# Sixteen-token projections: from one product of 256 columns to four of 64 in separate column groups of the array

## Chip, cores and metric

One NeuronCore of one Trainium2 chip runs the whole program. The metric is device time in microseconds (us), the median of several executions; one execution was also profiled. The work is done by TensorE (the 128x128 matrix array), VectorE, ScalarE and GpSimd; SyncE issues the transfers. In the profile these are PE, DVE, ACT, POOL and SP.

## What is computed

A batch of one with 256 tokens of width 1024 in float32 runs through two transformer blocks. The first block puts 16 learned "meta" tokens ahead of the 256, so that it works on 272 tokens, and has two layers. Each layer normalises the tokens, multiplies them by one wide input matrix, runs three kinds of attention (latent attention with 8 heads, stick-breaking attention with 8 heads, differential attention with 4 heads), merges them through gates, and ends with a feed-forward part. The second block has an attention mixer, a delta-rule mixer and two mixtures of 64 experts. The change touches only some projections of the first block:

```python
proj = h @ w_in[layer]
(c_q, c_kv, k_rope, sb_q, sb_k, sb_v,
 df_q, df_k, df_v, gate_logits) = _split_cols(proj, IN_SIZES)
```

The parts `sb_v` (the values of the stick-breaking attention) and `df_q`, `df_k`, `df_v` (queries, keys and values of the differential attention) are 512 columns wide each, and are the ones computed with tokens on the partitions.

## The kernel before

**Layout.** Activations lie as H[128 features, 8 blocks of features, 272 tokens]. The tokens are cut into three tiles, `TILES = [(0, 16), (16, 128), (144, 128)]`: the first tile is the 16 meta tokens (`META = 16`). Weights are streamed from memory in slots of 1 MB, each 256 output columns wide for all 1024 features, through a ring of four slots (`wdense`), which SyncE fills in a fixed order as TensorE is done with them.

**Two kinds of projection.** `feature_steps` (line 511) makes weights stationary and streams the tokens, and gives features on the partitions; the gates use it. `token_steps` (line 527) makes the tokens stationary and streams the weights, and gives tokens on the partitions. For each slot it goes through the three tiles of tokens. For each tile it takes a PSUM bank and runs 8 products (one for each block of 128 features), which accumulate into `o[0:n, 0:256]` (line 533, through `sum_k`, line 502). For the tile of 16 tokens the stationary operand is 128x16 and the moving one 128x256. In the trace each product in float32 is a pair of MATMULs with a LDWEIGHTS each, so this tile is 16 MATMULs "128*16 128x256". (A row of the timeline that shows x32 of them merges a 16-token tile and the tile of 128 tokens behind it, under the shape of the first.) Below, one such tile of one slot is called a *16-token step*.

**How many.** `sb_v`, `dq`, `dk` and `dv` take two slots each, so a layer has 8 such steps and the program has 16. The later mixers call `token_steps` with tiles of 128 tokens only.

**Who takes the results out.** The two tiles with an even number (the 16 tokens among them) are copied out of PSUM by VectorE in `even_tokens` (line 1327), the odd one by ScalarE in `odd_tokens`. `bank` (line 479) makes TensorE wait until the bank's last reader is through; eight banks rotate.

**The order of the work.** It is written out by hand, as generators that each engine advances alike. These projections are laid beside the attention heads, to fill TensorE while VectorE and ScalarE work on the probabilities. For head h of the latent attention, TensorE computes the scores of head h, advances the list `beside` by `BESIDE_MLA[h]` steps, and then transposes and applies the probabilities of head h-1. The two 16-token steps of `sb_v` come with heads 0 and 3. The stick-breaking heads do the same with `BESIDE_SB = (4, 4, 4, 4, 4, 5, 5, 6, 6)` over this list (`beside_sb`, line 347):

```python
yield from in_turn((dq, 6), (dk, 6), (rope_dq, 1), (gate, 1), (dv, 1), (gate, 1), (rope_dq, 1), (dv, 1), (gate, 1),
                   (dv, 1), (rope_dq, 1), (gate, 1), (dv, 1), (rope_dk, 1), (gate, 1), ...
```

So the 16-token steps of `dq` both come with head 0, the two of `dk` with heads 1 and 2, the first of `dv` with head 3, the second of `dv` with head 5. `rope_dq` and `rope_dk` are work of VectorE and ScalarE (the normalisation and rotation of DQ and DK, `norm_rope`, lines 1335 to 1362); TensorE does nothing in them.

**Applying probabilities.** `apply_v` (line 554) transposes the probabilities of a head (line 477), waits for VectorE to copy the 16-token part out of PSUM (`turned`, line 1378) and for ScalarE to copy the rest (line 2215), and then multiplies by the values.

Of the kernel before, what the change touches and what calls it, by code (L numbers as in the profile page):

```python
# [17 lines left out]
META = 16  # L18
# [5 lines left out]
TILES = [(0, META), (META, P), (META + P, P)]  # L24
# [212 lines left out]
def build(nc, io, out_ap, known):  # L237
    te, ve, ac, po, sp = nc.tensor, nc.vector, nc.scalar, nc.gpsimd, nc.sync
# [36 lines left out]
    def flat(a, n, *dims):  # L275
        ap = a[:, 0:n]
        if len(dims) == 1:
            return ap.rearrange("p (a b) -> p a b", a=dims[0])
        if len(dims) == 2:
            return ap.rearrange("p (a b c) -> p a b c", a=dims[0], b=dims[1])  # L280
        return ap
# [23 lines left out]
    def ps(*what):  # L305
        return PS[:, bank_of.get(what, 0), :]
# [18 lines left out]
    SVT = flat(wm_flat[:, 8 * T:], 1536, 3, 8)  # L325
# [15 lines left out]
    def in_turn(*order):  # L341

        for steps, n in order:
            for _ in range(n):
                yield next(steps, None)
# [117 lines left out]
    def tensor_program():  # L463
        PE, VE, AC = PES[0], VES[0], ACS[0]
# [6 lines left out]
        def mm(out, lhsT, rhs, start=True, stop=True):  # L471
            return te.matmul(out, lhsT, rhs, start=start, stop=stop, skip_group_check=True)  # L472
# [6 lines left out]
        def bank(what, *readers):  # L479

            while turn[0] % 8 in held:
                turn[0] += 1
            b = turn[0] % 8
            turn[0] += 1
            for done, label in owed[b]:
                te.wait_ge(done.sem, done.of(*label))
            owed[b] = [(done, what) for done in readers]
            assert what not in bank_of, what
            bank_of[what] = b
            return PS[:, b, :]  # L490

        def take(k, w):
            n = uses[0]
            uses[0] += 1
            te.wait_ge(*dense.landed(n))
            return dense.slot(n, k, w)

        def used(n=None):

            dense_at[uses[0] - 1 if n is None else n] = (PES.index(PE), PE.n)  # L500

        def sum_k(out, lhs, rhs, more=True):
            for j, (a, b) in enumerate(zip(lhs, rhs)):
                m = mm(out, a, b, start=j == 0, stop=j == len(lhs) - 1)
            return m
# [21 lines left out]
        def token_steps(what, src, kc, tiles, n_slots, readers, step=256):  # L527
            for s in range(n_slots):
                use, slot = uses[0], take(kc, step)
                for t, (t0, n) in enumerate(tiles):  # L530
                    label = what + (s, t)
                    o = bank(label, readers(t))
                    PE.up(sum_k(o[0:n, 0:step], [src[:, k, t0:t0 + n] for k in range(kc)],
                                [slot[:, k, :] for k in range(kc)]), *label)
                    if t == len(tiles) - 1:
                        used(use)
                    yield
# [36 lines left out]
        def first_layer(L):  # L574
# [27 lines left out]
            used()  # L602
            sb_qk = feature_steps(("sb qk", L), H, DC, T, 4, lambda j: AC)
            sb_v = token_steps(("sb v", L), H, DC, TILES, 2, lambda t: reader(t))
            gate = feature_steps(("gate", L), H[:, :, lo:T], DC, T - lo, 12, lambda j: AC if j < 2 else reader(j))
            advance(sb_qk, 1)
# [53 lines left out]
            def turned_to_feature(what, TMt, roped):  # L660
                te.wait_ge(VE.sem, VE.of("roped", roped, L))
                yield from to_feature((what, L), TMt.rearrange("p t h d -> p t (h d)"), 4, 128, lambda g: reader(g))

            tokens = lambda what: token_steps((what, L), H, DC, TILES, 2, lambda t: reader(t))
            beside = beside_sb(tokens("dq"), tokens("dk"), tokens("dv"), no_products(), no_products(), gate,
                               turned_to_feature("dqt", DQ, "dq"), turned_to_feature("dkt", DK, "dk"))
# [143 lines left out]
        def even_mixer():  # L810
# [70 lines left out]
            def moba():  # L881
# [31 lines left out]
                for h in range(4):  # L913
# [8 lines left out]
            run(even_order(gla(), moba(), norm_heads(("gla",), 1, [E_MIX[:, 4:8, :]]),  # L922
                           feature_steps(("mq",), H, DC, S, 2, both), feature_steps(("mk",), H, DC, S, 2, both),
                           token_steps(("mv",), H, DC, T2, 2, both), token_steps(("gv",), H, DC, T2, 2, both),
                           feature_steps(("gg",), H, DC, S, 2, both)))

# [368 lines left out]
        PE, VE, AC = PES[1], VES[1], ACS[1]  # L1295
# [3 lines left out]
        PE, VE, AC = PES[2], VES[2], ACS[2]  # L1299
# [4 lines left out]
    def vector_program():  # L1304
        PE, VE, AC = PES[0], VES[0], ACS[0]
# [5 lines left out]
        def copy(what, dst, src):  # L1311
            ve.wait_ge(PE.sem, PE.of(*what))
            VE.up(ve.tensor_copy(dst, src), *what)  # L1313
# [10 lines left out]
                    copy(what + (c,), *dst(c, ps(*what, c)))  # L1324
                yield

        def even_tokens(what, n_slots, tiles, dst):
            for s in range(n_slots):
                for t, (t0, n) in enumerate(tiles):
                    if t % 2 == 0:  # L1330
                        copy(what + (s, t), *dst(s, t, ps(*what, s, t)[0:n, 0:256]))
                    yield

# [63 lines left out]
        def first_layer(L):  # L1397
# [54 lines left out]
            for g in range(0, 8, 2):  # L1452
                copy(("kt", L, g), KT[0:96, g, :], ps("kt", L, g)[0:96, 0:T])

            sb_v = even_tokens(("sb v", L), 2, TILES, lambda s, t, o: (
                SVT[0:TILES[t][1], t, 4 * s:4 * s + 4, :], o.rearrange("p (h d) -> p h d", h=4)))
            beside = in_turn((sb_v, 3), (gate, 1), (sb_v, 3), (gate, 5))
            for h in range(MLA_H + 1):
                if h < MLA_H:
                    p, s = WA[h % 2], 10 * (h % 2)  # L1460
# [11 lines left out]

            def put(what, dst):
                fl = dst.rearrange("p t h d -> p t (h d)")
                return even_tokens((what, L), 2, TILES, lambda s, t, o: (fl[0:TILES[t][1], t, 256 * s:256 * s + 256], o))

            beside = beside_sb(
                put("dq", DQ), put("dk", DK), put("dv", DV),
                norm_rope("dq", DQ, row("diff_q_norm_g", 64 * L, 64 * L + 64), 64, 0, cst("df_cos"), cst("df_sin"), ROPE_D, L),
                norm_rope("dk", DK, row("diff_k_norm_g", 64 * L, 64 * L + 64), 64, 0, cst("df_cos"), cst("df_sin"), ROPE_D, L),  # L1480
# [5 lines left out]
            for h in range(SB_H + 1):  # L1486
                if h < SB_H:
                    z, e, lk, a = [WA[4 * (h % 2) + j] for j in range(4)]
                    what = ("sb", L, h)
# [46 lines left out]
            for br in range(3):  # L1536
                ve.wait_ge(AC.sem, AC.of("gates", L, br))
                for c in range(8):
                    what = ("branch", L, br, c)
                    o = ps(*what)[:, lo:T]  # L1540
# [9 lines left out]
            for c in range(8):  # L1550
                what = ("attended", L, c)
# [103 lines left out]
        def even_mixer():  # L1655
# [114 lines left out]
            def heads():  # L1770
# [9 lines left out]

            run(even_order(gla(), moba(), heads(), even_steps(("mq",), 4, fm(E_MQ)), even_steps(("mk",), 4, fm(E_MK)),
                           even_tokens(("mv",), 2, T2, tm(E_MV)), even_tokens(("gv",), 2, T2, tm(E_GV)), even_steps(("gg",), 4, fm(E_GG))))
            mix_out(0, "even out")
            layer_norm("even ln", modulated(0, "moe h", 0))
# [399 lines left out]
        for L in range(DEPTH):  # L2184
            first_layer(L)
# [10 lines left out]
        PE, VE, AC = PES[1], VES[1], ACS[1]  # L2196
# [3 lines left out]
        PE, VE, AC = PES[2], VES[2], ACS[2]  # L2200
# [738 lines left out]
```

## Time and profile before

| | |
|---|---|
| three timed runs | 3070.38, 3071.52 and 3080.09 us, median 3071.52 us |
| the profiled execution | 3072.53 us |
| its span, first to last instruction | 3071.2 us |
| mean granted TensorE clock | 0.968 of 2.4 GHz |
| TensorE matmul busy | 94% of the span, 16294 MATMULs |
| VectorE, ScalarE busy | 36%, 16% |

The profile is one execution. Times in it count from the first instruction. A row of the timeline gives the start, the length, the engine, the line, the operands and the number of instructions merged in it; in brackets stands how long the engine was idle before it, and what it waited for. "128*16 128x256" is a stationary operand of 128 rows and 16 columns against 256 moving columns.

### The profile page before, as it was taken

What the parts mean: (1) busy time and instruction counts of PE and PEld (TensorE: products, weight loads), DVE (VectorE), ACT (ScalarE), POOL (GpSimd) and SP (SyncE); (2) the same over time, 40 slices, a digit from 0 to 9 for tenths busy, and PEclk for the clock granted to TensorE, in tenths of its full rate; (3) what the DMA queues carried; (4) which work ended last, traced back from release to release, by engine and by line L of the source; (5) the groups of instructions that cost most, each with busy time, mean ns of one, the idle gap of its engine ahead of it and who ended that gap; (6) DMA issues with size and microseconds to landing.
All of it is one profiled execution on the core that took longest, in us unless ns stands there. A gap on an engine that the chain in (4) does not pass through costs nothing.

```text
span 3071.2 us, 41806 instructions
## 1 busy us (share of the span) xinstructions
PE 2883.4 (94%) x16294; PEld 2040.4 (66%) x16294; DVE 1115.9 (36%) x2516; ACT 487.2 (16%) x1066; POOL 102.7 (3%) x98
## 2 busy tenths in 40 slices
PE   7998899999999889999999999999899999999998
PEld 5666678787666678887875555555788765555554
DVE  2425424442534433543335222222564244222223
ACT  2212221000212221000211111111232111111111
POOL 0000000000000000000001000000000010000000
PEclk9998899999999899999999999999999889999999
DMA  5221135654221135664518999999231349999995
GB/s 187 82 82 69 55 123 208 248 214 149 96 83 69 69 110 213 233 240 178 214 70 334 394 399 382 400 402 390 101 124 57 123 185 403 402 405 399 400 403 218
DMA packets 104983, 684.45 MB, mean 223 GB/s; under 512 B 17760, under 2 KB 19312, under 8 KB 24496
## 3 DMA queue, kind: packets, MB, share of 16 engines
q1 hardware_dynamic: 93040, 665.02, 55.4%
q0 software_dynamic: 11264, 16.54, 1.5%
q8 instruction: 75, 1.23, 0.2%
q10 hardware_dynamic: 576, 1.43, 0.1%
q14 instruction: 28, 0.23, 0.0%
HBM read 703.37 MB, written 4.19 MB: 230 GB/s over the span
## 4 chain that ended last, share of the span: by engine, by line
PE 81%; DMA 11%; DVE 4%; ACT 2%; issue 1%; SPq 0%; DVEq 0%; ACTq 0%; POOLq 0%
PE PS L472 77%; DMA wmoe<-in_experts 10%; PE PS L477 4%; ACT AR L2215 1%; ACT AR L2265 1%; DMA COLS<-in_cols 0%; SPq L2823 0%; DVE ST L1371 0%; ACT ST L2215 0%; DVE X L1628 0%; DMA AR<-tokens,IX 0%; DVE AR L1521 0%; DVE AR L1368 0%; DVE wmoe L1391 0%; DVE AR L1519 0%
## 5 line engine op out<-in xcount | busy, mean ns | idle before, releaser
L472 PE MATMUL PS<-wmoe,AR 128*64 128x256 f32 (+2 forms) x5488 | 723.0, 420 | 35.7 <-DMA wmoe<-in_experts 22.5
L472 PE MATMUL PS<-H,wdense 128*128 128x256 f32 (+1 forms) x3056 | 719.6, 396 | 6.8 <-DVE H L1401 3.5
L472 PEld LDWEIGHTS PS<-H,wdense 128*128 128x128 f32 x3056 | 589.4, 195 | 116.2 <-issue 13.1
L472 PEld LDWEIGHTS PS<-wmoe,AR 128*64 128x64 f32 (+1 forms) x5488 | 388.9, 137 | 322.7 <-issue 148.3
L2215 ACT ACTIVATE AR<-PS 128x512 f32<-128x512 f32 (+7 forms) x497 | 227.1, 462 | 1624.5 <-PE PS L472 1023.8
L472 PE MATMUL PS<-AR,wdense 128*128 128x256 f32 (+1 forms) x1920 | 440.7, 389 | 21.3 <-DVE X L1591 6.4
L472 PE MATMUL PS<-AR 128*128 128x512 f32 (+16 forms) x1636 | 402.3, 395 | 40.3 <-DVE AR L1378 16.1
L472 PEld LDWEIGHTS PS<-AR,wdense 128*128 128x128 f32 x1920 | 367.4, 192 | 87.6 <-issue 20.4
L472 PEld LDWEIGHTS PS<-AR 128*128 128x128 f32 (+5 forms) x1636 | 214.0, 186 | 140.9 <-issue 92.6
L477 PEld LDWEIGHTS PS<-CST,AR 128*128 128x128 f32 (+3 forms) x1150 | 129.5, 134 | 159.5 <-issue 137.8
L472 PE MATMUL PS<-wdense,H 128*128 128x256 f32 (+4 forms) x1024 | 225.2, 376 | 2.5 <-DVE H L1635 2.2
L472 PEld LDWEIGHTS PS<-wdense,H 128*128 128x128 f32 (+1 forms) x1024 | 162.1, 171 | 56.7 <-issue 11.6
L477 PE MATMUL PS<-CST,AR 128*128 128x128 f32 (+3 forms) x1150 | 188.2, 275 | 6.0 <-DVE AR L2166 3.2
L1391 DVE SCALAR_TENSOR_TENSOR wmoe<-wmoe,CA 128x256 f32<-128x256 f32 x336 | 162.9, 485 | 12.0
L2129 DVE TENSOR_TENSOR AR<-AR,PS 128x256 f32<-128x256 f32 x67 | 28.2, 422 | 376.4 <-ACT AR L2215 376.4
L2135 DVE COPY AR<-PS 128x512 f32<-128x512 f32 x130 | 89.9, 692 | 135.1 <-PE PS L472 135.1
L2733 POOL DMA_INDIRECT AR<-tokens,IX x71 | 79.9, 1126 | 1056.0 <-DVE IX L2055 1005.5
L2215 ACT ACTIVATE AR<-AR 128x432 f32<-128x432 f32 (+8 forms) x111 | 76.7, 706 | 172.2 <-DVE AR L1491 83.9
L2119 DVE TENSOR_SCALAR AR<-AR 64x256 f32<-64x256 f32 x134 | 55.1, 411 | 104.3 <-PE PS L477 95.3
L1313 DVE COPY AR<-PS 128x256 f32<-128x256 f32 (+8 forms) x79 | 35.3, 448 | 152.6 <-PE PS L472 121.8
L472 PE MATMUL PS<-AR,CST 128*128 128x256 f32 (+4 forms) x212 | 62.3, 429 | 27.7 <-DMA COLS<-in_cols 15.9
L2215 ACT ACTIVATE AR<-X 128x256 f32<-128x256 f32 (+3 forms) x54 | 22.6, 462 | 346.5 <-DVE X L1591 132.9
(271 smaller groups left out, 1399.7 us busy)
## 6 DMA issues: line engine op xcount, KB each, us to landing
wmoe<-in_experts SPq DMA_DIRECT2D x402, 1024.0 KB, 9.0
wdense<-in_dense SPq DMA_DIRECT2D x176, 1024.0 KB, 4.8
wmoe<-in_ada SPq DMA_DIRECT2D x48, 1024.0 KB, 6.9
tokens<-AR POOLq DMA_DIRECT2D x4, 512.0 KB, 2.9
wdense<-in_dense SPq DMA_DIRECT2D x2, 768.0 KB, 10.5
wdense<-in_dense SPq DMA_DIRECT2D x2, 640.0 KB, 6.3
CST<-in_const SPq DMA_DIRECT2D x1, 1197.0 KB, 19.2
AR<-tokens,IX POOLq DMA_INDIRECT x71, 7.8
```

The source lines that it names most:

```text
L472: return te.matmul(out, lhsT, rhs, start=start, stop=stop, skip_group_check=True)
L477: return te.matmul(out, src, ident[0:n, 0:n], start=True, stop=True, is_transpose=True, skip_group_check=True)
L1313: VE.up(ve.tensor_copy(dst, src), *what)
L1391: VE.up(ve.scalar_tensor_tensor(ACC[:, s], WM[:, s, 256 * k:256 * k + 256], CA[:, k:k + 1], ACC[:, s], ALU.mult, ALU.add))
L2119: VE.up(ve.tensor_scalar(M_PWT[half].rearrange("p t s -> p (t s)"), M_NUM[half], M_IW[half, bass.ds(p, 1), 0], M_IW[half, bass.ds(p, 1), 1 ...
L2129: VE.up(ve.tensor_tensor(M_HM, M_HM, PS[:, B_GU, 0:256], ALU.mult))
L2135: VE.up(ve.tensor_copy(M_YE[:, q, :], PS[:, B_D[q], :]), *what, "ye", q)
L2215: return ac.activation(dst, src, f, bias=bias, scale=scale)
L2265: AC.up(ac.activation(p[:, o:o + w], p[:, o:o + w], Exp, bias=ST[:, s + j:s + j + 1], scale=1.0, accum_out=ST[:, s + 3 + j:s + 4 + j]))
L2733: po.indirect_dma_start(M_XT, None, tokens[L], bass.IndirectOffsetOnAxis(M_IX[:, column:column + 1], 0), bounds_check=SEQ - 1, oob_is_err= ...
```

## The change

For a tile of 16 tokens, the product with 256 weight columns becomes four products with 64 columns each. Product a writes its 16 rows at PSUM partitions 32a to 32a+15, that is from the a-th group of 32 columns of the array, and at columns 0 to 63 of the bank. The stationary operand (the 16 tokens) is loaded for each of them. Within each block of features the four follow one another. VectorE then takes the result out with four copies of 16x64, one from each range of partitions, where it had one of 16x256; they land in the same places as before. The tiles of 128 tokens and all else stay as they were.

```diff
@@ token_steps
-                    PE.up(sum_k(o[0:n, 0:step], [src[:, k, t0:t0 + n] for k in range(kc)],
-                                [slot[:, k, :] for k in range(kc)]), *label)
+                    if n == META:
+                        for k in range(kc):
+                            for a in range(4):
+                                m = mm(o[32 * a:32 * a + n, 0:step // 4], src[:, k, t0:t0 + n], slot[:, k, step // 4 * a:step // 4 * (a + 1)],
+                                       start=k == 0, stop=k == kc - 1)
+                        PE.up(m, *label)
+                    else:
+                        PE.up(sum_k(o[0:n, 0:step], [src[:, k, t0:t0 + n] for k in range(kc)],
+                                    [slot[:, k, :] for k in range(kc)]), *label)
@@ even_tokens, in the vector program
-        def even_tokens(what, n_slots, tiles, dst):
+        def even_tokens(what, n_slots, tiles, dst, quarter=None):
...
-                    if t % 2 == 0:
+                    if n == META:
+                        ve.wait_ge(PE.sem, PE.of(*what, s, t))
+                        for a in range(4):
+                            VE.up(ve.tensor_copy(quarter(s, a), ps(*what, s, t)[32 * a:32 * a + n, 0:64]))
+                        VE.mark(*what, s, t)
+                    elif t % 2 == 0:
                         copy(what + (s, t), *dst(s, t, ps(*what, s, t)[0:n, 0:256]))
@@ its callers
-                SVT[0:TILES[t][1], t, 4 * s:4 * s + 4, :], o.rearrange("p (h d) -> p h d", h=4)))
+                SVT[0:TILES[t][1], t, 4 * s:4 * s + 4, :], o.rearrange("p (h d) -> p h d", h=4)), lambda s, a: SVT[0:META, 0, 4 * s + a, :])
...
-                return even_tokens((what, L), 2, TILES, lambda s, t, o: (fl[0:TILES[t][1], t, 256 * s:256 * s + 256], o))
+                return even_tokens((what, L), 2, TILES, lambda s, t, o: (fl[0:TILES[t][1], t, 256 * s:256 * s + 256], o),
+                                   lambda s, a: fl[0:META, 0, 256 * s + 64 * a:256 * s + 64 * (a + 1)])
```

## Rows read from the trace of the kernel before

**Rows 1.** The page's chain that ended last, share of the span by engine.

```profile
PE 81%; DMA 11%; DVE 4%; ACT 2%; issue 1%; SPq 0%; DVEq 0%; ACTq 0%; POOLq 0%
```

**Rows 2.** Groups of matmuls by shape, whole span: count | busy us, mean ns | idle before.

```profile
L472 PE MATMUL PS<-wmoe,AR 128*64 128x256 f32 x4288 | 477.7, 381 | 1.5 <-ACT AR L2215 1.4
L472 PE MATMUL PS<-H,wdense 128*128 128x256 f32 x1792 | 411.0, 389 | 1.6 <-DVE H L1562 1.6
L472 PE MATMUL PS<-wdense,H 128*16 128x256 f32 x256 | 59.7, 388 | 0.0
```

**Rows 3.** TensorE's timeline beside latent head 3 and stick-breaking heads 0 and 1, layer 0.

```profile
123.13 7.28 PE L472 MATMUL PS<-wdense,H 128*16 128x256 f32 x32
130.25 0.97 PE L477 MATMUL PS<-CST,AR 128*16 128x128 f32 x6
...
175.93 15.97 PE L472 MATMUL PS<-wdense,H 128*16 128x256 f32 x64
191.83 1.10 PE L472 MATMUL PS<-wmoe 64*128 64x272 f32 x6
...
207.07 0.97 PE L477 MATMUL PS<-CST,AR 128*16 128x128 f32 x6
```

**Rows 4.** TensorE's timeline of both later mixers: 64-column products in several parts of the array.

```profile
1469.37 0.47 PE L472 MATMUL PS<-AR 64*64 64x64 f32 x16
1469.77 3.72 PE L472 MATMUL PS<-wdense,H 128*128 128x256 f32 x16
...
2282.38 3.95 PE L472 MATMUL PS<-AR 128*64 128x64 f32 x128
```

**Rows 5.** VectorE's copies out of PSUM by shape, whole span.

```profile
L2056 DVE COPY AR<-PS 128x3 f32 x55 | 8.9, 161 | 0.0
L1313 DVE COPY AR<-PS 16x256 f32<-16x256 f32 x13 | 5.3, 408 | 15.5 <-PE PS L472 15.5
```

**Rows 6.** Timeline beside stick-breaking head 3: VectorE, ScalarE in layer 0; VectorE, ScalarE in layer 1.

```profile
239.89 0.40 DVE L1313 COPY AR<-PS 16x256 f32<-16x256 f32 x1
241.55 0.43 DVE L1378 COPY AR<-PS 16x272 f32<-16x272 f32 x1 [1.26 <-PE PS L477]
...
240.74 0.49 ACT L2215 ACTIVATE wmoe<-PS,COLS 128x272 f32<-128x272 f32 x1 [0.57 <-PE PS L472]
241.55 0.49 ACT L2215 ACTIVATE AR<-PS 128x384 f32<-128x384 f32 x1 [0.32 <-PE PS L477]
...
957.37 0.43 DVE L1378 COPY AR<-PS 16x272 f32<-16x272 f32 x1 [2.54 <-PE PS L477]
...
956.57 0.47 ACT L2215 ACTIVATE wmoe<-PS,COLS 128x256 f32<-128x256 f32 x1 [1.84 <-PE PS L472]
```

**Rows 7.** Timeline beside stick-breaking head 5, layer 0: TensorE, VectorE, ScalarE.

```profile
263.14 3.63 PE L472 MATMUL PS<-wdense,H 128*16 128x256 f32 x16
...
275.67 2.60 PE L472 MATMUL PS<-AR,wmoe 16*64 16x272 f32 x6 [4.23 <-ACT AR L2215]
...
259.38 0.61 DVE L1491 TENSOR_SCALAR AR<-PS 128x432 f32<-128x432 f32 x1 [0.58 <-PE PS L472]
...
271.16 0.41 DVE L1313 COPY AR<-PS 16x256 f32<-16x256 f32 x1
272.79 1.75 DVE L1340 TENSOR_REDUCE wmoe<-wmoe 128x24 f32<-128x1536 f32 x1 [1.23 <-ACT wmoe L2215]
...
275.06 0.47 ACT L2215 ACTIVATE AR<-PS 128x384 f32<-128x384 f32 x1
```

**Rows 8.** The page's DMA issues: count, KB each, median us to landing.

```profile
wdense<-in_dense SPq DMA_DIRECT2D x176, 1024.0 KB, 4.8
```

**Rows 9.** Windows; columns: length, PE, PEld, DVE, ACT, POOL busy, clock, DMA, GB/s.

```profile
99.00:176.00 77.00, 71.09 (x343) 50.29 (x344) 25.72 (x83) 16.57 (x61) 0.43 (x1) 1.00 0.19 68
176.00:229.00 53.00, 51.66 (x231) 35.01 (x232) 16.77 (x29) 9.32 (x18) 2.27 (x2) 0.97 0.22 77
...
276.00:301.00 25.00, 19.24 (x68) 14.11 (x66) 13.85 (x16) 3.59 (x7) 0.00 (x0) 0.77 0.22 84
```

## Prediction

> **What bounds the kernel now.** The page comes first: TensorE is busy for 94% of the span, and the chain that ended last runs through it for 81% [rows 1]. Then the matmuls by shape: the 16-token steps are the 256 MATMULs of 128*16 against 128x256, 59.7 us busy [rows 2]. That is all the change can remove from TensorE, 1.9% of the span; whether a step's share reaches the end is read from the stretch it stands in.
>
> The timeline of TensorE gives the length of a step. With latent head 3, 32 MATMULs start at 123.13 and the next work at 130.25 [rows 3]: 7.12 us, 0.2225 us for each, and a step of 16 takes 3.56 us. The stretch from 99 to 176 us (latent heads, two steps) has VectorE busy 25.72 us of 77 and ScalarE 16.57; from 176 to 229 us (stick-breaking heads 0 to 2, four steps) it is 16.77 and 9.32 of 53, while TensorE is busy 71.09 and 51.66 [rows 9]. The transposes at 130.25 and 207.07 start with no idle time before them [rows 3], so the probabilities were ready. These six steps of a layer are bound by TensorE.
>
> The two steps of dv are different. Beside head 3, VectorE ends the 16-token copy at 240.29 and then waits 1.26 us for the transposes; ScalarE starts the gate it has to take out after 0.57 us of idle time, at 240.74, and its copy at 241.55 follows 0.32 us of idle time [rows 6]. So VectorE and ScalarE are only about 1 us ahead there. In layer 1 the same waits are 2.54 us and 1.84 us [rows 6]. Beside head 5, TensorE itself waits: 4.23 us until 275.67, for ScalarE's copy at 275.06 [rows 7]. The chain behind that copy begins with VectorE's work on the scores at 259.38, goes through the rotation of DQ and ends with VectorE's sum at 272.79 and ScalarE's work behind it [rows 7]. The 16-token step at 263.14 lies inside this chain's time, hidden.
>
> **The change part by part.** *Removed:* 16 MATMULs a step, 3.56 us.
>
> *Added:* 64 MATMULs a step, each a quarter as wide. What they take depends on how far the four groups of columns work at once, and no row shows four groups with all 128 rows. The bounds: a pass of 256 columns takes 0.2225 us, so one of 64 takes 0.056 us. One after another, 64 take 3.56 us: nothing gained. In four groups fully side by side they take 64 x 0.014 = 0.89 us. Between the ends stand two rows. With two groups (64 stationary columns each) 128 MATMULs of 64 columns take 3.95 us [rows 4], less a latency of 0.22 us for the last (the 0.47 us and the 0.40 us of the other row and the wide matmuls' 0.38 us all contain one) about 29 ns each. With four parts of the array (two groups of rows by two of columns) 16 MATMULs start at 1469.37, and the next tile's first MATMUL starts at 1469.77 [rows 4]: 0.40 us for all 16, the start and the hand-over included, where a serial array would need 0.9 us. And in the experts' products two groups of columns side by side take 477.7/4288 = 0.111 us a MATMUL against 411.0/1792 = 0.229 us for the full array at the same 256 columns [rows 2], exactly a half. I take the four-part row, since the change too has four parts: 0.40 us for the first 16 and 48 x 0.014 = 0.67 us for the rest, 1.07 us a step. Saved: 3.56 - 1.07 = 2.49 us. The fourfold loading of the 16 tokens is in that figure, since every MATMUL of the row has its own load, with more columns than here.
>
> By the page "TensorEngine Tiling (Array Packing)" of the Trainium skill, section Instruction Overhead, each matmul has an overhead of some 60 cycles, so that a factor should not be taken from a dimension that is already small; 64 columns are just there. The Trainium skill's page "TensorE: Matmul & The Clock Gate", section Wait — 56ns, not 53.3ns?, has a floor of about 25 ns from start to start. By 25 ns a step is at least 64 x 25 = 1.6 us. The 16 MATMULs in 0.40 us do not show such a floor, but they are few.
>
> *VectorE:* a copy of 16x256 takes 408 ns and one of 128x3 161 ns [rows 5], 0.98 ns a column, so one of 16x64 takes 0.22 us. In the rows, neighbours that need no wait overlap by 0.08 us (the copy at 239.89 follows a gate that started at 239.48). Four take 4 x 0.14 + 0.08 = 0.64 us, 0.23 us more than one. In the six first steps VectorE's idle time hides it (two thirds of the stretch). Beside head 5 the copy at 271.16 is followed by 1.23 us of idle time [rows 7], which takes it as well. Beside head 3 it counts. Bounds: nothing, and four full copies less one, 0.5 us.
>
> *Beside head 3* TensorE gains at most what the others are ahead. In layer 0 VectorE has 1.26 - 0.23 = 1.03 us; ScalarE has 0.57 + 0.32 = 0.89 us; the step gives 0.9 us. In layer 1 VectorE has 2.54 - 0.23 = 2.3 us, ScalarE 1.84 + 0.3 = 2.1 us: 2.1 us. *Beside head 5* the step gives nothing: TensorE's wait of 4.23 us grows to 6.7 us.
>
> *Sum:* 12 steps x 2.49 = 29.9 us, plus 0.9 + 2.1 = 3.0, is 32.9 us. The rest is unchanged: the weights of a slot land in 4.8 us [rows 8], and a slot's three tiles still take 2 x 3.56 + 1.07 = 8.2 us, with four slots in the ring; TensorE's later work starts that much earlier and meets no fixed time, since the experts' loads too are released by its own progress. The longer wait beside head 5 costs no clock by itself: behind the present one the clock is 0.77 from 276 to 301 us [rows 9], which is already the lower of the two levels, 1.2 GHz, for about half of it, and how long the engine idles before it came back changes nothing in these rows. But each stretch at the lower level may fall elsewhere; I allow 2 us either way.
>
> The profiled execution took 3072.53 us (span 3071.2), 1.0 us over the median of 3071.52. Against it the sum gives 3039.6; against the median, 3038.6.
>
> **The rivals.**
>
> *A pace per MATMUL.* TensorE may not take up 64-column products faster than about 29 ns for long, whatever their groups. For it: no run of more than 16 in the trace is faster [rows 4]. Against it: those 16. A step would then take 64 x 0.029 + 0.15 = 2.0 us and save 1.56; with 12 x 1.56 + 0.9 + 1.56 = 21.2 us the time is 3050. By the 25 ns of the Trainium skill ("TensorE: Matmul & The Clock Gate", as above), a step of 1.75 us with the hand-over, it would be 3047.
>
> *The groups don't overlap.* If the four products of a block are worked off in order, each after the one before, the step stays at 3.6 us and the change does not do what it is built for: 3072, no change. Against it stand the two-group rows, where one group's work runs beside the other's in just this order of issue.
>
> *A change of group drains the array.* If a product has to wait until the one before has left the array, as long as a matmul's latency of 0.22 us, then the 32 products of a step take 32 x (0.056 + 0.22) = 8.8 us, 5.3 us more than before. Fourteen steps on the path give 74 us and the two beside head 5 some 1 us each over their wait: 3147. It decides once a product with its two passes takes over 0.13 us, where a step is 0.66 us longer than now. The two-group rows change group at every product and show nothing of it.
>
> *VectorE takes over.* If its copies were much dearer, from partitions 32, 64 and 96 to partition 0, or if ScalarE and VectorE turned out late beside heads 0 to 2 too, half of the gain could stay in waits: 3055.
>
> **How the numbers follow.** The forecast has a chance of 0.64, the pace 0.17, VectorE 0.06, no overlap 0.09, the drain 0.04. A measurement of this kernel can tell 0.3%, 9 us. Faster by more than that: 0.64 + 0.17 + 0.06 = 0.87; the same 0.09; slower 0.04. The range reaches down to 3033 (a step of 0.89 us for twelve gives 2 us more, the clock 2, a little beside head 3) and up to 3053, which holds the pace rival with the clock's 2 us; what lies outside is about 0.2.
>
> **What would show it.** In the profile after: 64 MATMULs of 128*16 128x64 a step, 1024 in all; with latent head 3, 4.6 us where 7.12 stood; a step alone close to 1.1 us. A step near 2.0 us speaks for the pace, 3.6 us for no overlap, over 4.2 us for the drain. Beside head 3 of layer 0 TensorE's wait for ScalarE's copy should be about 2.2 us, and beside head 5 about 6.7 us. VectorE's copies should be 16x64, about 0.22 us. The forecast is wrong if the steps are that short and the time is not down by some 30 us: then a wait stands in the stretches from 99 to 229 us where none is expected.

## The result, and the profile after

The changed kernel takes 3042.43 us (median of 5 runs, 3039.18 to 3049.91) where the kernel before took 3070.38 us (5 runs, 3066.77 to 3080.09) beside it: 28.0 us less, a ratio of 0.9911 with a 95% interval of 0.9889 to 0.9934. The forecast was 3038.6 us in a range of 3033 to 3053. The profiled execution took 3047.81 us (span 3046.5, clock 0.965), near the upper end of its runs; against the profiled execution of before it is 24.7 us shorter, so a sum made from the two traces has to come to 24.7.

First the groups by shape over the whole span, for the products and the copies [rows 2, 5].

```profile
L472 PE MATMUL PS<-wdense,H 128*16 128x64 f32 x1024 | 17.4, 220 | 0.0
...
L1341 DVE COPY AR<-PS 16x64 f32<-16x64 f32 x48 | 10.4, 216 | 2.4 <-PE PS L472 1.2
...
L1341 DVE COPY wmoe<-PS 16x64 f32<-16x64 f32 x16 | 3.5, 216 | 0.4
```

There are 1024 MATMULs, busy 17.4 us, where 256 were busy 59.7 us. One of them takes 220 ns from start to end, as a 64-column MATMUL of 64*64 did in the kernel before (218 ns); it is their starts that lie close. In the trace they come four at a time, within some 20 ns, and the next four start 56 ns after the first. TensorE's timeline beside latent head 3, and then beside stick-breaking head 3 of layer 0 and of layer 1, answers to [rows 3, 6]:

```profile
121.75 4.74 PE L472 MATMUL PS<-wdense,H 128*16 128x64 f32 x80
126.32 0.86 PE L477 MATMUL PS<-CST,AR 128*16 128x128 f32 x5
...
217.44 1.09 PE L472 MATMUL PS<-wdense,H 128*16 128x64 f32 x64
218.46 3.93 PE L472 MATMUL PS<-H,wdense 128*128 128x272 f32 x16
222.23 0.97 PE L477 MATMUL PS<-CST,AR 128*16 128x128 f32 x6
225.58 2.14 PE L472 MATMUL PS<-AR,wmoe 16*64 16x272 f32 x6 [2.39 <-DVE AR L1391]
227.65 1.99 PE L472 MATMUL PS<-wmoe 64*128 64x272 f32 x6
229.58 5.39 PE L472 MATMUL PS<-wdense,H 128*128 128x256 f32 x16
234.81 3.83 PE L472 MATMUL PS<-H,wdense 128*128 128x272 f32 x16
...
919.57 1.09 PE L472 MATMUL PS<-wdense,H 128*16 128x64 f32 x64
920.58 3.72 PE L472 MATMUL PS<-H,wdense 128*128 128x256 f32 x16
...
927.91 1.46 PE L472 MATMUL PS<-AR,wmoe 16*64 16x272 f32 x6 [2.80 <-DVE AR L1391]
929.30 1.99 PE L472 MATMUL PS<-wmoe 64*128 64x272 f32 x6
931.22 6.14 PE L472 MATMUL PS<-wdense,H 128*128 128x256 f32 x16
937.20 3.62 PE L472 MATMUL PS<-H,wdense 128*128 128x256 f32 x16
```

A 16-token step now runs from 217.44 to 218.46, 1.02 us, and with latent head 3 a step and the wide tile behind it end after 4.57 us (121.75 to 126.32), where 7.12 stood. Beside head 3 the wait for the probabilities, 0.67 us in the kernel before, is 2.39 and 2.80 us, and what follows it is slower than it was: six scores take 1.99 us and the next 16 MATMULs of 128x256 take 5.39 and 6.14 us. In the kernel before the same rows, in layer 0, read:

```profile
242.18 1.43 PE L472 MATMUL PS<-AR,wmoe 16*64 16x272 f32 x6 [0.67 <-ACT AR L2215]
243.55 1.09 PE L472 MATMUL PS<-wmoe 64*128 64x272 f32 x6
244.57 3.72 PE L472 MATMUL PS<-wdense,H 128*128 128x256 f32 x16
248.13 3.83 PE L472 MATMUL PS<-H,wdense 128*128 128x272 f32 x16
```

From the end of the wait to the second projection tile behind it, it was 5.95 us (242.18 to 248.13) and is 9.23 us (225.58 to 234.81), 3.3 more. In layer 1 it was 5.94 us and is 9.29 (927.91 to 937.20), 3.3 more again.

The windows give the granted clock of TensorE (the figure behind POOL's; 1.00 is 2.4 GHz and 0.50 the lower level, 1.2 GHz): before the new wait, behind it in layer 0, and behind it in layer 1.

```profile
217.30:225.50 8.20, 5.89 (x87) 4.44 (x86) 5.77 (x11) 3.34 (x6) 0.00 (x0) 1.00 0.26 80
225.50:233.00 7.50, 7.42 (x20) 5.38 (x21) 1.40 (x4) 1.78 (x3) 0.00 (x0) 0.54 0.13 55
...
928.00:937.00 9.00, 9.00 (x28) 6.89 (x29) 3.62 (x6) 1.78 (x3) 0.00 (x0) 0.62 0.05 19
```

The clock goes from 1.00 to 0.54 in the 7.5 us behind the wait: the lower level of 1.2 GHz for nearly all of it. Before the change the windows at this place show 1.00 (238 to 246 and 246 to 256 us). VectorE's timeline of layer 0 shows who was last, and what the four copies take:

```profile
222.03 1.75 DVE L1353 TENSOR_REDUCE wmoe<-wmoe 128x24 f32<-128x1536 f32 x1 [2.20 <-ACT wmoe L2229]
223.71 0.49 DVE L1457 TENSOR_SCALAR wmoe<-PS,COLS 128x272 f32<-128x272 f32 x1
224.11 0.95 DVE L1341 COPY AR<-PS 16x64 f32<-16x64 f32 x4
225.10 0.43 DVE L1391 COPY AR<-PS 16x272 f32<-16x272 f32 x1
```

The copy that TensorE waits for (`turned`, now line 1391) ends at 225.53, and TensorE goes on at 225.58; ScalarE had ended its own copy at 225.15.

Beside head 5 of layer 0 TensorE waits 6.77 us, where it waited 4.23 [rows 7]: the 2.54 us of that step went into the wait, as forecast.

**The account.** The two traces were laid over each other, MATMUL by MATMUL, in the stretch of attention (from a layer's first latent scores to its first differential scores): 463.2 us before and 438.3 after in both layers together, 24.8 less, all of the 24.7 of the whole. Each of the 12 first steps gives 2.54 us (30.5). The step beside head 3 gives 2.54 less the growth of the wait, 0.82 us in layer 0 and 0.41 in layer 1 (1.2). Behind the two longer waits 3.3 us each are lost again (6.6): that is 6.8 us at half the clock each time. Other stretches at the lower clock came and went between the two executions (three of 3.4 us at 176, 876 and 944 us of the kernel before; one of 6.8 us at 854 and one of 3.4 us at 899 of the kernel after) and cancel. From the end of the wait beside head 5 on, layer 0 gains 1.0 us and layer 1 loses 1.3 (-0.3). 30.5 + 1.2 - 6.6 - 0.3 = 24.8.

### The profile page after: what moved, and what is told of

It is laid out like the page before. It is cut to its first block, busy times and chain, and to the rows that moved or that the text cites. A ratio compares the mean times of both kernels' runs of the same rounds, so it can differ in the third digit from the quotient of the medians.

```text
span 3046.5 us, 43390 instructions
## 1 busy us (share of the span) xinstructions
PE 2851.9 (94%) x17062; PEld 2040.3 (67%) x17062; DVE 1123.0 (37%) x2564; ACT 486.8 (16%) x1066; POOL 102.7 (3%) x98
## 4 chain that ended last, share of the span: by engine, by line
PE 81%; DMA 10%; DVE 5%; ACT 2%; issue 1%; SPq 0%; DVEq 0%; ACTq 0%
PE PS L472 77%; DMA wmoe<-in_experts 10%; PE PS L477 4%; ACT AR L2229 1%; ACT AR L2279 1%; DMA COLS<-in_cols 0%; SPq L2837 0%; DVE ST L1384 0%; ACT wmoe L2229 0%; ACT ST L2229 0%; DVE X L1642 0%; DVE wmoe L1353 0%; DVE AR L1535 0%; DVE AR L1381 0%; DVE wmoe L1404 0%
## 5 line engine op out<-in xcount | busy, mean ns | idle before, releaser
L472 PE MATMUL PS<-wdense,H 128*16 128x64 f32 (+4 forms) x1792 | 188.3, 289 | 3.4 <-DVE H L1649 3.4
L472 PEld LDWEIGHTS PS<-wdense,H 128*16 128x16 f32 (+1 forms) x1792 | 156.4, 141 | 28.3 <-issue 6.7
L472 PE MATMUL PS<-AR,wmoe 64*64 64x64 f32 (+3 forms) x448 | 46.7, 277 | 37.6 <-ACT AR L2229 20.7
## 6 DMA issues: line engine op xcount, KB each, us to landing
wdense<-in_dense SPq DMA_DIRECT2D x2, 768.0 KB, 10.2
```

## Experiments

Three questions: what carries the short step (the groups, or only the narrower products); whether the part of the change in `dv` costs more than it gives, through the wait beside head 3; and whether filling the holes (the waits of TensorE) with other work recovers it. A *pass* below is one MATMUL streaming its columns through the array; a *group* is one of the four groups of 32 columns of the array. Unless said otherwise an edit is made to the changed kernel. "Stretch" is the stretch of attention of both layers, as above, in the profiled execution. What lies outside it, where no edit reaches, took 2603 to 2618 us in the profiled executions of all kernels that compute the same tokens. So the stretch tells differences of a few us that the time of the whole does not. The kernel before had medians of 3070.18, 3069.81 and 3070.15 us beside the three sets of runs.

### All steps but those of dv

```diff
-                    if n == META:
+                    if n == META and what[0] != "dv":
```

(in `token_steps` and in `even_tokens`)

> The 16-token steps of sb_v, dq and dk in four groups as in the changed kernel, those of dv wide as before. Theory A (the steps on TensorE's path give 2.54 us each, and the new wait beside head 3 drops the clock, which costs 2.7 to 3.3 us a layer against 0.9 and 2.1 us that the step gives there): TensorE's wait beside head 3 is back at 0.67 us, the clock stays high in layer 0 from 225 to 240 us, and the whole is 12 x 2.54 = 30 us under the kernel before, 2 to 3 us under the changed kernel. Rival B (the clock would have fallen anyway, the shortfall is scatter): the dv steps are worth their 3 us, and this kernel is 27 us under the one before at best, 3 us over the changed one's 30.

Measured: 3045.17 us, ratio 0.9914 (0.9888 to 0.9939). Stretch 434.3 us, 4.0 less than with all sixteen steps in groups. TensorE's timeline of layer 0 behind head 3, and the window there:

```profile
226.19 1.43 PE L472 MATMUL PS<-AR,wmoe 16*64 16x272 f32 x6 [0.67 <-ACT AR L2229]
227.55 1.09 PE L472 MATMUL PS<-wmoe 64*128 64x272 f32 x6
228.58 3.72 PE L472 MATMUL PS<-wdense,H 128*128 128x256 f32 x16
...
226.00:242.00 16.00, 15.14 (x71) 11.74 (x72) 8.78 (x11) 3.15 (x7) 0.00 (x0) 1.00 0.25 89
```

The wait is back at 0.67 us, the clock stays at 1.00 there, in layer 1 as well, and the whole is as fast as with the dv steps changed, within what the intervals separate. By its median it is 25.0 us under the kernel before, where the changed kernel is 28.0 under: the 3 us less that the rival expected. The stretch goes the way of the theory, and the intervals don't decide between the two. What can be said is that the four steps of dv bring nothing that these times can tell, and cost 4.0 us in the stretch of the profiled pair, little more than chance alone makes there (3.2 us between two executions of one kernel, at the end of this section).

### Only the steps of dv

```diff
-                    if n == META:
+                    if n == META and what[0] == "dv":
```

> The complement of e1: only the four steps of dv in four groups, sb_v, dq and dk wide as before. Theory A: beside head 3 TensorE waits 2.4 us (layer 0) for VectorE and ScalarE, and the clock falls behind that wait; beside head 5 the wait grows from 4.23 to 6.8 us and gives nothing. The stretch of attention (from the first latent scores to the first differential scores, both layers, 463.2 us before) is 0 to 5 us longer than before. Rival B (the dv steps beside head 3 are worth their 0.9 and 2.1 us): it is 3 us shorter.

Measured: 3075.83 us, ratio 1.0017 (0.9996 to 1.0039). Stretch 469.1 us, 6.0 longer than in the kernel before. TensorE's timeline beside head 3, in layer 0 and in layer 1:

```profile
248.01 1.46 PE L472 MATMUL PS<-AR,wmoe 16*64 16x272 f32 x6 [2.38 <-DVE AR L1391]
249.40 1.09 PE L472 MATMUL PS<-wmoe 64*128 64x272 f32 x6
250.43 5.41 PE L472 MATMUL PS<-wdense,H 128*128 128x256 f32 x16
...
961.02 2.63 PE L472 MATMUL PS<-AR,wmoe 16*64 16x272 f32 x6 [2.80 <-DVE AR L1391]
963.58 1.99 PE L472 MATMUL PS<-wmoe 64*128 64x272 f32 x6
965.50 6.39 PE L472 MATMUL PS<-wdense,H 128*128 128x256 f32 x16
```

The same waits to 0.01 us, and again slower rows behind both: 3.4 us at the lower clock in layer 0 and 10.2 in layer 1, where the changed kernel had 6.8 and 6.8. Four steps, each 2.54 us shorter, make the stretch longer, by 1.0 us more than was expected at most. The time of the whole doesn't show a loss: its interval takes in 1.

### One group, and what the mark of a start does

The four products of 64 columns side by side in the bank, all in the array's first group, and one copy of 16x256:

```diff
-                                m = mm(o[32 * a:32 * a + n, 0:step // 4], src[:, k, t0:t0 + n], slot[:, k, step // 4 * a:step // 4 * (a + 1)],
+                                m = mm(o[0:n, step // 4 * a:step // 4 * (a + 1)], src[:, k, t0:t0 + n], slot[:, k, step // 4 * a:step // 4 * (a + 1)],
```

> Four products of 64 columns as in the changed kernel, but all in the first group of columns (they write columns 64a to 64a+63 of the bank on the same 16 partitions, and VectorE takes them out with one copy as before). Theory A (the gain is the groups working at once): 64 MATMULs at 56 to 58 ns, a step of 3.6 to 3.8 us, the whole within 4 us of the kernel before. Rival C (the narrow product itself is cheaper, the groups don't matter): a step near 1 us and some 28 us less.

Measured: 3057.59 us, ratio 0.9947 (0.9928 to 0.9966), yet a step of 3.68 us:

```profile
233.10 3.75 PE L472 MATMUL PS<-wdense,H 128*16 128x64 f32 x64
236.78 1.41 PE L472 MATMUL PS<-H,wdense 128*128 128x272 f32 x5
```

Here each of the four products marks the start of a sum in the same bank and partitions. The tokens change by it, the experts get other tokens, and their MATMULs of 128x512 are 1056 where the other kernels have 1072. The time of the whole is that of other work, and only the step's length counts. By the Trainium skill ("PSUM — Partial Sum Buffer", The four PSUM rules) a start clears the `has_written` bits of the whole bank in the quadrants of partitions that are written. By that rule the next product of an earlier quarter overwrites instead of adding, and for three quarters of the columns the first block of 128 features is left out of the sum. The other tokens of this run agree; which columns are off was not read apart. The run was repeated with the start marked on the first of the four alone:

```diff
-                                       start=k == 0, stop=k == kc - 1)
+                                       start=k == 0 and a == 0, stop=k == kc - 1)
```

> e2 again (all four products of 64 columns in the first group of columns), but only the first product of a step marks the start of its accumulation; e2 marked it on each of the four, and computed other sums (the flag of the start seems to reach the whole bank on these partitions, so that the first block of features was lost for three quarters of the columns), so that the experts got other tokens and e2's total can't be compared. Theory A: a step of 3.68 us as in e2, 0.12 us longer than the wide one; the stretch of attention within 2 us of the 463.2 us before, and the whole within 4 us.

Measured: 3074.18 us, ratio 1.0012 (0.9994 to 1.003). With one mark the experts' MATMULs are 1072 again. The step from one start to the next:

```profile
240.71 3.75 PE L472 MATMUL PS<-wdense,H 128*16 128x64 f32 x64
244.38 1.87 PE L472 MATMUL PS<-H,wdense 128*128 128x272 f32 x7
```

3.67 us: 64 passes 0.057 us apart. The stretch is 465.7 us, 2.6 more than before where within 2 was expected, and the whole 4.4 us more by the medians, with an interval that takes in no change. Narrow products alone give nothing, and with the fourfold loading they cost 0.1 us a step; the gain is the groups' alone.

### Two groups of 128 columns

```diff
-                            for a in range(4):
-                                m = mm(o[32 * a:32 * a + n, 0:step // 4], src[:, k, t0:t0 + n], slot[:, k, step // 4 * a:step // 4 * (a + 1)],
+                            for a in range(2):
+                                m = mm(o[32 * a:32 * a + n, 0:step // 2], src[:, k, t0:t0 + n], slot[:, k, step // 2 * a:step // 2 * (a + 1)],
```

(and two copies of 16x128)

> Two products of 128 columns in two groups, two copies of 16x128. Theory A: 32 MATMULs, two at a time, 16 x 0.109 = 1.75 us and 0.15 us for the hand-over, a step of 1.9 us, 1.65 us saved; twelve steps give 20 us, the step beside head 3 about 0.9 and 1.6 us; with the wait there at 1.7 us instead of 2.4 the clock may hold. Whole: 20 to 23 us under the kernel before. Rival (a pace per MATMUL bounds the four-group step): the two-group step is no longer than the four-group one.

Measured: 3055.22 us, ratio 0.995 (0.993 to 0.997).

```profile
251.84 1.93 PE L472 MATMUL PS<-wdense,H 128*16 128x128 f32 x32
253.70 2.56 PE L472 MATMUL PS<-H,wdense 128*128 128x272 f32 x10
```

A step takes 1.86 us. With one, two and four groups it is 3.67, 1.86 and 1.02: the passes of a single group (64 of 0.056 us, 16 of 0.111 and 16 of 0.056) and about 0.1 us of hand-over, whatever the number of MATMULs. That is no pace per MATMUL, which would have made the four groups' 64 dearer than the two groups' 32.

The whole is 15.0 us under the kernel before, where 20 to 23 were expected. The stretch, 441.1 us, is 22.0 shorter, so the missing us lie outside it, in work that the edit does not touch. Beside head 3 the wait is 0.67 us in layer 0 and 1.67 in layer 1, where the clock falls 1.7 us behind it:

```profile
929.92 1.43 PE L472 MATMUL PS<-AR,wmoe 16*64 16x272 f32 x6 [1.67 <-DVE AR L1391]
932.89 6.46 PE L472 MATMUL PS<-wdense,H 128*128 128x256 f32 x16
```

### The four groups one after the other

```diff
-                        for k in range(kc):
-                            for a in range(4):
+                        for a in range(4):
+                            for k in range(kc):
```

> The same 32 products in four groups, but the loop over groups outside and that over the 8 blocks of features inside, so that 16 MATMULs in a row use one group. Theory A with a short look-ahead (in the trace of before, a product in another part of the array starts some 4 to 8 MATMULs ahead of its turn): groups overlap only where one ends and the next begins, a step of 2.0 to 3.5 us, and most of the gain goes. Rival D (TensorE sees the whole step ahead, the order does not matter): a step of 1.0 us and 28 us less, as in the changed kernel.

Measured: 3067.96 us, ratio 0.9991 (0.9973 to 1.0009).

```profile
231.58 3.13 PE L472 MATMUL PS<-wdense,H 128*16 128x64 f32 x64
234.64 2.56 PE L472 MATMUL PS<-H,wdense 128*128 128x272 f32 x10
```

A step takes 3.06 us: the same 64 MATMULs in the same four groups save 0.5 us instead of 2.54. A group's sixteen passes hold up the next group's, but for some 0.17 us at each of three hand-overs, three passes. The single starts in the trace show the same: a group's first MATMUL starts when three of the sixteen of the group before it are still to start. So TensorE looks only a few MATMULs ahead, and the order of issue in the change is a part of its gain.

In layer 1 this run has a stretch of 3.4 us at the lower clock behind a wait beside head 3 of only 0.75 us:

```profile
947.35 1.46 PE L472 MATMUL PS<-AR,wmoe 16*64 16x272 f32 x6 [0.75 <-DVE AR L1391]
949.77 5.41 PE L472 MATMUL PS<-wdense,H 128*128 128x256 f32 x16
```

### Other work in the holes

To the changed kernel, a gate (`gate`, some 4 us of TensorE, taken out by VectorE or ScalarE) moved from head 7 to head 3, and one from head 8 to head 5:

```diff
-    BESIDE_MLA, BESIDE_SB, BESIDE_DF = (2, 1, 1, 2, 1, 1, 2, 1, 1), (4, 4, 4, 4, 4, 5, 5, 6, 6), (2, 1, 1, 1, 1)
+    BESIDE_MLA, BESIDE_SB, BESIDE_DF = (2, 1, 1, 2, 1, 1, 2, 1, 1), (4, 4, 4, 5, 4, 6, 5, 5, 5), (2, 1, 1, 1, 1)
...
-        yield from in_turn((dq, 6), (dk, 6), (rope_dq, 1), (gate, 1), (dv, 1), (gate, 1), (rope_dq, 1), (dv, 1), (gate, 1),
-                           (dv, 1), (rope_dq, 1), (gate, 1), (dv, 1), (rope_dk, 1), (gate, 1), (rope_dk, 1), (dv, 1), (gate, 1),
-                           (dv, 1), (rope_dk, 1), (gate, 2), (dqt, 4), (gate, 2), (dkt, 4))
+        yield from in_turn((dq, 6), (dk, 6), (rope_dq, 1), (gate, 1), (dv, 1), (gate, 2), (rope_dq, 1), (dv, 1), (gate, 1),
+                           (dv, 1), (rope_dq, 1), (dv, 1), (gate, 1), (rope_dk, 1), (gate, 2), (rope_dk, 1), (dv, 1), (gate, 1),
+                           (dv, 1), (rope_dk, 1), (gate, 1), (dqt, 4), (gate, 1), (dkt, 4))
```

> The changed kernel, with one step of the gates moved from beside stick-breaking head 7 to head 3 and one from head 8 to head 5 (in head 5 the dv step stands ahead of the gate, to keep the order of the slots). Theory A: the gate's 3.8 us beside head 3 takes up the wait of 2.4 us and keeps the clock, the one beside head 5 stands in the wait of 6.8 us; both heads 7 and 8 lose 3.8 us. The stretch of attention is 434 - 2 x 3.5 = 420 to 430 us against 438.3 us in the changed kernel, the whole 8 to 18 us under it. Rival B (the waits and the clock are not what holds the time): no difference beyond 3 us.

Measured: 3031.24 us, ratio 0.9861 (0.9837 to 0.9885), stretch 419.0 us. TensorE's timeline beside heads 3 and 5 of layer 0:

```profile
230.72 1.43 PE L472 MATMUL PS<-AR,wmoe 16*64 16x272 f32 x6 [0.67 <-ACT AR L2229]
...
264.58 2.61 PE L472 MATMUL PS<-AR,wmoe 16*64 16x272 f32 x6 [3.68 <-ACT AR L2229]
```

The wait beside head 3 is back at 0.67 us and the clock holds behind it, in both layers, with the dv steps still in four groups: so the form of these steps alone does not bring the lower clock. The time is 10.6 us further under the kernel before than the changed kernel's was, within the 8 to 18 of the theory and beyond the rival's 3; the stretch is 1.0 us shorter than expected.

The same move in the kernel before, where the wait beside head 3 is not there to fill:

> The kernel before with the same gates moved and the products wide. Theory A: beside head 3 nothing is to be filled, so that the moved gate gives nothing there; beside head 5 it fills 3.8 of the 4.23 us of wait, and the clock holds: 3.3 us and up to 3 us of clock a layer, a stretch of 451 to 457 us against 463.2, the whole 6 to 12 us under the kernel before. So the change to four groups is worth more with the gates moved (some 30 us between this and e6) than without (27 us).

Measured: 3065.52 us, ratio 0.9981 (0.9963 to 0.9999), stretch 456.9 us, 6.3 less than the 463.2 of before. The stretch is as expected; the whole is only 4.3 us less, where 6 to 12 were expected. With the change the same move takes the stretch from 438.3 to 419.0, 19.3 us, and the ratio from 0.9911 to 0.9861. Some of this is the clock: 44.4 us of the stretch lie at the lower level where 68.3 did. A us at half the clock costs half a us, so this is worth 12 us of the 19.

### A third gate

From head 7 to head 5, into the 3.68 us left there, with the version with two moved run again beside it:

```diff
-    BESIDE_MLA, BESIDE_SB, BESIDE_DF = (2, 1, 1, 2, 1, 1, 2, 1, 1), (4, 4, 4, 5, 4, 6, 5, 5, 5), (2, 1, 1, 1, 1)
+    BESIDE_MLA, BESIDE_SB, BESIDE_DF = (2, 1, 1, 2, 1, 1, 2, 1, 1), (4, 4, 4, 5, 4, 7, 5, 4, 5), (2, 1, 1, 1, 1)
```

(and the list `beside_sb` to match)

> The kernel with one gate more moved: head 5 now starts three gates (the one moved from head 8 and one from head 7), head 3 two, heads 7 and 8 one less each; all steps of sixteen tokens in four groups. Theory (the wait is a hole in TensorE's cover, and a hole brings cold clock behind it): beside head 5 a wait of 3.68 us was left in the version with two gates moved; another gate of 4 us fills it, so that wait falls to 1 us or less and the clock behind it holds. The stretch of attention of both layers comes out at 409 to 418 us, where two gates moved gave 419.0, and the whole at 3022 to 3030. Rival (the chain through VectorE and ScalarE sets head 5's end, and a gate there only moves TensorE's wait to head 7, which has one gate fewer): the wait beside head 5 goes, one of 2 to 4 us appears beside head 7, and the whole is the same as with two moved, 3028 to 3035.

> The version with two gates moved once more, on the same chip as the one with three, to compare them: 3031 within 6 us, a stretch of attention of 419 within 4 us in both layers together (both theories).

Measured: three moved 3021.66 us, ratio 0.9851 (0.9827 to 0.9876); two moved 3027.4 us, ratio 0.9869 (0.9851 to 0.9887). TensorE's timeline of three moved, beside heads 5, 6 and 7 of layer 0:

```profile
265.31 1.43 PE L472 MATMUL PS<-AR,wmoe 16*64 16x272 f32 x6 [0.67 <-ACT AR L2229]
...
285.10 2.64 PE L472 MATMUL PS<-AR,wmoe 16*64 16x272 f32 x6 [5.75 <-DVE AR L1391]
...
297.54 2.61 PE L472 MATMUL PS<-AR,wmoe 16*64 16x272 f32 x6 [3.17 <-ACT AR L2229]
```

In layer 0 the wait beside head 5 is gone (in layer 1 it is 1.22 us), and the clock holds behind it in both, as the theory had it. But a wait of 3.17 us stands beside head 7, where the gate was taken from: the rival's mechanism. From about the end of the wait beside head 6 the clock now stays at the lower level for 20.5 us, where two moved gates had 10.2. The stretches are 415.4 and 415.8 us, the same. The medians differ by 5.7 us, in the direction of the theory, but the intervals overlap: whether three are better than two stays open. Either is faster than both kernels of this case. The run of two moved also shows how much of a stretch is chance: the same kernel had 419.0 us with 44.4 at the lower clock, and now 415.8 with 37.5.

## Why the prediction was right, and where it was not

**The step.** The sum had 1.07 us from the row with four parts of the array; 1.02 was measured, 12 x 0.05 = 0.6 us better. The bound worked out for four groups fully side by side, 0.89 us, is what the passes take, and the rest is hand-over. The rival of a pace per MATMUL falls with the step itself (64 MATMULs in 1.02 us, 0.016 us each) and with two groups; so does, across groups, the floor of about 25 ns from start to start in the Trainium skill ("TensorE: Matmul & The Clock Gate", Wait — 56ns, not 53.3ns?). Whether it holds within one group was not tried: the passes there are 0.056 us apart. No overlap and the drain fall with the step too. Something near no overlap (0.5 us saved) was measured only where the sixteen MATMULs of a group were issued in a row.

**Six first steps of a layer bound by TensorE.** Right: each gives its whole 2.54 us, and no new wait stands in those stretches.

**VectorE's copies.** One takes 0.216 us, as forecast, but the four take 0.95 us and not 0.64, since neighbours don't overlap here; 0.55 us more than the one of 0.40. This shows beside head 3, where VectorE, and not ScalarE, is what TensorE now waits for. In layer 0 its 1.26 us of slack less 0.55 leaves 0.71, against 0.82 measured and 0.9 forecast.

**Beside head 3 of layer 1.** Forecast 2.1 us, measured 0.41. The 2.54 us that VectorE waited there were read as its slack. In TensorE's timeline of the kernel before, just ahead of them, stands

```profile
943.92 5.41 PE L472 MATMUL PS<-H,wdense 128*128 128x256 f32 x16
949.25 3.63 PE L472 MATMUL PS<-wdense,H 128*16 128x256 f32 x16
```

that is, 16 MATMULs that take 3.72 us elsewhere took 5.41, in a stretch of 3.4 us at the lower clock. 1.69 us of the wait were TensorE's lateness in this one execution: 2.54 - 1.69 - 0.55 = 0.30 is what was left, near the 0.41. Two other kernels bear this out: in layer 1 the wait takes all but 0.41 us of the 2.54 with only dv in groups, and all but 0.42 of the 0.50 with the groups one after the other. So layer 1 had no more slack than layer 0; in that one execution it only looked so.

**Beside head 5.** Right: 6.77 us for 6.7, nothing gained. That the length of the wait changes nothing in the clock behind it held in layer 0 (10.2 us at the lower level with the wait of 4.23 us and with that of 6.77) but not in layer 1 (10.2 us with 4.65, 13.7 with 7.20). From there on the two layers together lose 0.3 us, within the 2 us allowed.

**The clock: the step that failed.** The prediction went through what a longer wait costs beside head 5 only, priced it at nothing with 2 us either way, and put no price at all on the wait that it forecast itself beside head 3, about 2.2 us where there had been 0.67. Behind it the clock fell, in both layers, and again in both layers of the kernel with only dv changed (waits of 2.38 and 2.80 us); it did not fall there in the four executions where dv was left as it was or a gate filled the hole in the changed kernel (0.67 us each time, in both layers). The price is 3.3 us in each layer, more than the 0.8 and 0.4 that the steps give. Taken with the other terms, 32.9 + 0.6 - 1.8 - 6.6 - 0.3 is 24.8 for the profiled pair. The medians differ by 28.0, 3 us better; the runs of the changed kernel alone spread over 10.7 us, and how much of that is stretches at the lower clock falling elsewhere was not tried apart. The range held the time because its upper end was made for a slower step, not because the clock was in it; that the median missed the forecast by only 3.8 us is in part luck. The prediction's own sign of being wrong, a wait between 99 and 229 us of the kernel before, pointed to the wrong place: in the changed kernel no wait of TensorE before head 3 is longer than 0.67 us, and the loss stands behind head 3.

What ties the clock to the wait is that both came and went together. In the twelve profiled executions of this case, two layers each, the wait beside head 3 was 1.67 to 2.80 us in five places, and in all five a stretch at the lower level (3.4 to 10.2 us) began within 3 us of its end. It was 0.67 or 0.75 us in the other nineteen, and in eighteen of them none began in the next 10 us. The exception (layer 1 with the groups one after the other, 0.75 us) and the stretches that stand beside no long wait at all (176 and 944 us of the kernel before) show that a long wait is not the only way to it; by what rule the clock falls was not tried.

## What to carry to other kernels

A stationary operand of 16 columns leaves three of the four groups of columns idle: cut the moving columns in four, put each quarter in its own group, and issue the groups in turn within each block of the contraction; the step is then as long as one quarter's passes and 0.1 us. Before taking work off TensorE beside a chain of the other engines, ask what fills the hole, because a hole of two microseconds can cost three behind it; leave such a place alone or move other work into it in the same edit. And read slack from more than one layer: in a single execution part of it can be one stretch at the lower clock.

## What was not expected of the hardware

- Sixteen passes in each of four groups, with all 128 rows in use, run in 1.02 us, although in the order of issue the two passes of one product stand next to each other (the kernel issues a product as one instruction, which the trace shows as a pair). If every MATMUL had to start behind the one issued before it, the second pass of each of the 32 products would wait 0.056 us for the first, 1.8 us in all. If the pair is issued together, TensorE starts another group's MATMUL ahead of a waiting one. With sixteen passes of one group issued in a row the trace shows it directly, and that it reaches only a few ahead: the next group starts three passes early, and the step takes 3.06 us.
- Four marks of a start in one bank, on the same partitions, change the result (1056 MATMULs of the experts for 1072); one mark doesn't, and in groups with partitions of their own the four marks don't disturb each other.
- Four products in one group cost no more than one of four times the width but for 0.1 us a step, so the repeated loading of 16 columns hides behind passes of 0.056 us.
